# Two attentions and a mixture of experts: values placed ahead of transposes, rows split inside the head loop, scatter groups moved among products

## The reference, cut to what matters

```python
# neighbourhood attention, per head and row of the 4 x 64 grid
s = einsum(q_r, k_g) + bias
p = softmax(s)
o = einsum(p, v_g)          # 16 heads of 64; then o @ w_o
# latent attention, per head, all 256 keys
s = (q_nope . k_nope + q_rope . k_rope) * scale
o = softmax(s) @ v          # 16 heads of 64; then o @ w_o
# experts
for e in range(8):
    y = y + combine[:, e:e+1] * _swiglu(hf, w_gu[e], w_down[e])
```

## Time and profile before

| | us |
|---|---|
| median of 3 runs | 1655.73 (1654.92 to 1656.09) |
| the profiled execution, its own time | 1658.01 |
| its span, first to last instruction | 1656.2 |
| mean granted TensorE clock | 0.988 |
| PE busy | 1580.6 (95%) |
| DVE busy | 1203.5 (73%) |
| ACT busy | 866.1 (52%) |
| GpSimd busy | 116.6 (7%) |
| DMA, mean rate | 233 GB/s |

### The profile page before, as it was taken

The page is one execution under the profiler, slowest core; times in us unless marked ns, Lnnn a source line. Parts: engine busy times, 40 slices in busy tenths (PEclk is TensorE's granted clock), DMA queues, the critical chain, the costliest instruction groups (busy, mean ns, idle before and its releaser), DMA issues.

```text
span 1656.2 us, 24755 instructions
## 1 busy us (share of the span) xinstructions
PE 1580.6 (95%) x10292; PEld 1360.5 (82%) x10292; DVE 1203.5 (73%) x1428; ACT 866.1 (52%) x1009; POOL 116.6 (7%) x138
## 2 busy tenths in 40 slices
PE   7999999979999999998999999889999999999998
PEld 7999989867999989856999986578787877877876
DVE  5777769754777776455776763568888988988996
ACT  5333456443443354335434343457777677777765
POOL 0100012210000000151000002600000000000000
PEclk9999999999999999999999999999999999999999
DMA  8777634222687755404877740029998988988983
GB/s 330 276 283 263 252 105 150 71 77 76 264 324 284 297 212 177 154 1 169 304 257 279 267 178 1 1 102 351 342 344 314 375 312 317 364 323 308 365 327 134
DMA packets 51922, 386.32 MB, mean 233 GB/s; under 512 B 5888, under 2 KB 6224, under 8 KB 7904
## 3 DMA queue, kind: packets, MB, share of 16 engines
q1 hardware_dynamic: 50400, 376.16, 61.5%
q0 software_dynamic: 1408, 8.54, 1.4%
HBM read 383.63 MB, written 1.05 MB: 232 GB/s over the span
## 4 chain that ended last, share of the span: by engine, by line
PE 80%; DVE 9%; ACT 5%; issue 2%; POOL 2%; DMA 1%; DVEq 0%; ACTq 0%
PE bank L302 22%; PE bank L304 21%; PE bank L303 21%; PE bank L1286 4%; DVE sb_wlo L269 2%; PE bank L1861 1%; ACT sb_whi L265 1%; DVE sb_wlo L2288 1%; DMA sb_ada_raw<-in_ada 1%; PE bank L1820 1%; DVE sb_ada_acc L686 1%; PE bank L2016 1%; PE bank L696 1%; PE bank L540 1%; PE bank L1976 1%
## 5 line engine op out<-in xcount | busy, mean ns | idle before, releaser
L269 DVE TENSOR_TENSOR sb_wlo<-sb_raw,sb_whi 128x2048 fp32r<-128x2048 f32 x137 | 313.8, 2292 | 170.6 <-ACT sb_whi L265 170.4
L302 PE MATMUL bank<-sb_xhi,sb_whi 128*128 128x256 f32 x1344 | 382.8, 285 | 4.3 <-DVE sb_xlo L582 1.8
L303 PE MATMUL bank<-sb_xlo,sb_whi 128*128 128x256 f32 x1344 | 380.9, 283 | 0.0
L304 PE MATMUL bank<-sb_xhi,sb_wlo 128*128 128x256 f32 x1344 | 380.9, 283 | 0.0
L265 ACT ACTIVATE sb_whi<-sb_raw 128x2048 fp32r<-128x2048 f32 x137 | 261.5, 1909 | 177.1 <-PE bank L304 177.0
L302 PEld LDWEIGHTS bank<-sb_xhi,sb_whi 128*128 128x128 f32 x1344 | 258.5, 192 | 8.5 <-issue 4.0
L303 PEld LDWEIGHTS bank<-sb_xlo,sb_whi 128*128 128x128 f32 x1344 | 258.5, 192 | 1.1
L304 PEld LDWEIGHTS bank<-sb_xhi,sb_wlo 128*128 128x128 f32 x1344 | 258.5, 192 | 0.0
L2288 DVE TENSOR_TENSOR sb_wlo<-sb_raw,sb_whi 128x2048 fp32r<-128x2048 f32 x84 | 191.4, 2286 | 15.2 <-ACT sb_whi L2282 14.0
L302 PE MATMUL bank<-sb_whi,sb_slots_hi 128*128 128x512 f32 x448 | 181.5, 405 | 0.0
L304 PE MATMUL bank<-sb_whi,sb_slots_lo 128*128 128x512 f32 x448 | 176.3, 393 | 0.0
(11 more groups left out here) (462 smaller groups left out, 2492.3 us busy)
## 6 DMA issues: line engine op xcount, KB each, us to landing
sb_raw<-in_ffn SPq DMA_DIRECT2D x98, 1024.0 KB, 4.9
sb_raw<-in_moe SPq DMA_DIRECT2D x86, 1024.0 KB, 5.3
sb_ada_raw<-in_ada SPq DMA_DIRECT2D x32, 1536.0 KB, 6.3
sb_cst<-in_moe SPq DMA_DIRECT2D x28, 1024.0 KB, 5.1
sb_xn<-in_moe SPq DMA_DIRECT2D x27, 1024.0 KB, 5.2
sb_ada_raw<-in_moe SPq DMA_DIRECT2D x27, 1024.0 KB, 5.1
sb_raw<-in_w_in SPq DMA_DIRECT2D x13, 1024.0 KB, 4.8
sb_raw<-in_na_qk SPq DMA_DIRECT2D x8, 1024.0 KB, 5.3
```

Of the source, the lines that this page charges most:

```text
L269: e.tensor_tensor(wlo[s][:, :], raw[s][:, :], whi[s][:, :], ALU.subtract).then_inc(s_lo[s], 1)
L302: e.matmul(dst, wh, xh, start=first, stop=False, skip_group_check=skip)
L303: e.matmul(dst, wh, xl, start=False, stop=False, skip_group_check=skip)
L304: return e.matmul(dst, wl, xh, start=False, stop=last, skip_group_check=skip)
```

## The change

In both attentions `weigh(i - 3)` is put ahead of `transposed(i - 2)` in each iteration. The splitting of rows into high and low parts moves from behind the loop into it: k-tiles 0 to 5 in iterations 7, 11 and 15, the last two behind the loop. In the experts, piece 3 of the scatter moves behind `p_in(j + 1)` of k-steps 0 and 1 and `p_turn(j)`, and pieces 0 to 2 move behind k-steps 4 and 5. No operation is added or removed.

```diff
--- before.py
+++ after.py
@@ -324,15 +324,18 @@
             m = act.step(lambda e: e.activation(dst, src, ACT.Sqrt, bias=bias, scale=scale), *after)
             return dve.step(lambda e: e.reciprocal(dst, dst), m)
 
+        def split_pair(k, *after):
+
+            mh = act.step(lambda e: e.activation(xhi[:, k:k + 2, :], xn[:, k:k + 2, :], ACT.Copy), *after)
+            ml = dve.step(lambda e: e.tensor_tensor(xlo[:, k:k + 2, :], xn[:, k:k + 2, :], xhi[:, k:k + 2, :],
+                                                    ALU.subtract), mh)
+            return [ml, ml]
+
         def split_xn(m):
 
             parts = []
             for k in range(0, KT, 2):
-                mh = act.step(lambda e, k=k: e.activation(xhi[:, k:k + 2, :], xn[:, k:k + 2, :], ACT.Copy),
-                              *(m[k:k + 2] if isinstance(m, list) else (m,)))
-                ml = dve.step(lambda e, k=k: e.tensor_tensor(xlo[:, k:k + 2, :], xn[:, k:k + 2, :],
-                                                             xhi[:, k:k + 2, :], ALU.subtract), mh)
-                parts += [ml, ml]
+                parts += split_pair(k, *m[k:k + 2])
             return parts
 
         s_acc, s_sum, s_scaled = sem("accumulated"), sem("residual_added"), sem("gate_applied")
@@ -1867,17 +1870,23 @@
                 dst, src = order(dst), src.rearrange("p (r c) -> p r c", c=GRID)
             m_out[i // 2] = act.step(lambda e: e.activation(dst, src, ACT.Copy), m)
 
+    def split(n):
+        return env["split_pair"](2 * n, *[m_out[2 * n + z] for z in range(2)])
+
+    parts = []
     for i in range(AH + 3):
         if i < AH:
             softmax(i)
         if 0 <= i - 1 < AH:
             normalised(i - 1)
+        if 0 <= i - 3 < AH:
+            weigh(i - 3)
         if 0 <= i - 2 < AH:
             transposed(i - 2)
-        if 0 <= i - 3 < AH:
-            weigh(i - 3)
+        if i >= 7 and i % 4 == 3:
+            parts += split(i // 4 - 1)
         follow(i)
-    return [m_out[i] for i in range(AH // 2)]
+    return parts + split(AH // 4 - 1)
 
 
 def neighbourhood(env, early, m_in):
@@ -1939,7 +1948,6 @@
         m = attend(env, ctx, "na", scores, lambda i, kb: v[:, kb, i * HD:(i + 1) * HD], 1.0,
                    bias[:, :, :, :, :].rearrange("p b h r c -> p b h (r c)"), lambda i: [*m1, m_b, m_mask], follow, lambda i: (mask[i % 2 * HD:i % 2 * HD + HD, 0:P], mask[i % 2 * HD:i % 2 * HD + HD, P:P + T]),
                    lambda z: backwards(z.rearrange("p (r c) -> p r c", c=GRID)))
-        m = env["split_xn"](m)
         env["release"]()
     return env["project"](ch["na_o"], m, env["first"]["ffn3"]), kept[3]
 
@@ -2550,10 +2557,10 @@
             ex, u = j // EU, j % EU
             if gathers(j):
                 p_gather(e, *gathers(j))
+            p_in(e, j + 1, range(0, 2))
+            p_turn(e, j)
             if u == 1 and ex > 0:
                 p_scatter(e, ex - 1, (3,))
-            p_in(e, j + 1, range(0, 2))
-            p_turn(e, j)
             p_in(e, j + 1, range(2, 4))
             if u == 5:
                 p_keys(e, ex)
@@ -2564,9 +2571,10 @@
                 p_down(e, j, (1,))
                 p_down(e, j + 1)
                 break
+            p_in(e, j + 1, range(4, 6))
             if u == 0 and ex > 0:
                 p_scatter(e, ex - 1, (0, 1, 2))
-            p_in(e, j + 1, range(4, 8))
+            p_in(e, j + 1, range(6, 8))
             p_down(e, j)
         p_scatter(e, EXPERTS - 1, END)
```

## The result

The changed kernel takes 1637.07 us (median of 4 runs, 1635.96 to 1637.94); run beside it, the kernel before takes 1655.33 (1653.43 to 1656.09). The direction and most of the mechanisms came out; one mechanism, the price of the splits, did not, and the sizes were too small. One execution that fell in the chip's slower state (1740.4 at a granted clock of 0.843, of the kernel with two tensors on GpSimd) is left out of every median here.

The account below looks back on a forecast made before the run. TensorE, busy 95% of the span, was taken as the bound, so only its waits and slow stretches could be won. Attentions 6.2 plus experts 5.2 made 11.4 us, 1655.7 to 1644.3, range 1639 to 1650.

Parts of the forecast that it names:

- Values ahead, first attention: First attention: transposes no longer wait for GpSimd's normalisation in iterations 5, 7, 9, 11 and 13, 5 x 0.46 = 2.3 us.
- Values ahead, second attention: Second attention: the same waits gone, three pairs without gate rows 0.74 each, three with them 0.45 each, together 3.5 us.
- Tails: End of each attention: the projection starts 9.7 after head 15's scores instead of 10.68; 1.0 won twice, 2.0 us.
- Splits in the loop: Both attentions: inserted splits cost 1.6 us in all, DVE's low parts being held by GpSimd; bounds nothing and 9.8.
- Held until then, DVE is free at 5.06: First attention: low part held until GpSimd's normalisation ends at 4.37, DVE 0.99 late, transposes wait some 0.4 in iteration 13.
- 0.15 and 0.25: Last pair of heads in the attentions: costs counted because the reciprocal of head 15 comes late.
- Experts: Changes of expert: later scatter pieces win 1.0 in each of 4 without a gather, 0.4 in the others, 5.2 us.
- Both forecast waits: Experts: seven waits of 0.55, transposes for DVE's product, and three of about 1, gather for the addition.
- Rival (a): Experts: DVE isn't late, so 12.2 us won there and 1637.3 in all, 1641 with half the difference; chance 0.12.
- rival (d): Attention heads: changed rhythm holds PE at 1.2 GHz, so slower, 1686 us for a whole attention; chance 0.04.
- own bounds: Whole kernel: splits 0.5 to 4, pairs with gates 0 to 0.74, experts 3 to 8, giving 1640.5 to 1649 us.
- a wait behind iteration 11's split in the first attention: Transposes expected to wait 0.4 to 0.8 us two iterations behind the split of iteration 11.

Follow-up runs that it names:

- the kernel with two tensors on GpSimd: Changed kernel with GpSimd's normalisation as a product of two SBUF tensors instead of a product with a scalar per partition: 1637.06 us, ratio 0.9895.
- the run with values first only: Kernel before with only the values put ahead of the transposes, rows split behind the loop as before: 1651.23 us against 1654.19, ratio 0.9987.
- the run in which GpSimd's had that kind: Changed kernel with GpSimd's normalisation as a two-tensor multiplication, done twice for heads 6, 10 and 14: 1641.95 us, one run.
- the DVE order: Changed kernel with DVE's expert queue reordered: gate-up product ahead of piece 0's addition, piece 3's addition right behind pieces 1 and 2: 1637.49 us, ratio 0.9895.
- after again: Changed kernel run and profiled again with nothing else altered: 1637.02 us, ratio 0.9893.

## Why the prediction was wrong, step by step

It was wrong in size: 11.4 forecast, 14.6 in the traces, 18.3 between the medians. Its steps miss 3.2, the largest part being the splits; another 4 lie outside its steps, and these take the result out of the range. In the order of its steps:

- **Values ahead, first attention, 2.3.** 2.57. The three pairs without gate rows gave 0.46 each, as said; the two with them gave 0.6.
- **Values ahead, second attention, 3.5.** 4.37 (with the splits out of the way). Two terms were small: a pair without gates gave 0.89 and not 0.74, for PE's iteration turned out 2.46 and not the 2.55 counted, and pairs with gates gave 0.53 to 0.59 instead of 0.45.
- **Tails, 2.0.** 2.3. The reckoned 9.7 from the S of head 15 to the projection was 9.54 and 9.31.
- **Splits in the loop, 1.6 in all.** This is the step that failed by its mechanism. "Held until then, DVE is free at 5.06" did not happen: DVE's low part ran its 0.69 beside GpSimd's normalisation, six times of six. The low part, and the high part of ACT that it waits for, do delay what stands behind them on DVE: the reciprocal of head 11 comes 0.47 later than in the run with values first only in the first attention, where 0.60 is spare, and 0.64 later in the second. That of head 15 comes 1.06 and 0.90 later, right behind the low part, but T of head 15 stands behind a W that waits for a copy, and does not wait; 0.15 and 0.25 were counted for it. The nearest row was of another kind of GpSimd instruction (TENSOR_TENSOR in the mixer), and the run in which GpSimd's had that kind shows the hold. What was left of the cost is one wait of 0.26, with its restart 0.33, in iteration 13 of the second attention.
- **Experts, 5.2.** 5.65: 3 x 0.47 and 4 x 1.06, where 0.4 and 1.0 stood. Both forecast waits are there, in number and kind, 0.4 long and not 0.55. Rival (a) is excluded by them, and the DVE order shows what most of it would have been worth: 4.1 more.
- **The steps together** are 3.2 short: splits 1.3, second attention 0.9, tails 0.3, first attention 0.3, experts 0.4. With the traced 14.6 the forecast would have been 1641.1, inside the range.
- **The rest, 4.** The 58 runs of the kernel before beside the experiments have a median of 1654.6 and not 1655.7: 1.1. The whole change's runs had a mean clock of 0.9898 and before's 0.9879: 1.4 by the slope. Some 1.5 stay unexplained. The prediction weighed the granted clock only as a risk (rival (d), a whole attention at 1.2 GHz). It should have had a spread of 2 us to either side for it, which the "own bounds" left out. Rival (d) itself did not come: from head 5 to head 15 the granted clock is 1.00 in every profile. But the low stretch of the earlier trace rows is still there. In the window 700 to 710 the clock went from 0.66 to 0.86, only because the heads start 5.7 us earlier. Counted from the first S, the first 20 us of the heads have the same 0.83 in the first profile of the change as before, and 0.74 in the second.

Windows of 20 us from the first S: before, after, after again:

```profile
695.30:715.30 20.00, 16.25 (x66) 8.95 (x67) 8.25 (x39) 7.87 (x24) 10.39 (x11) 0.83 0.10 41
```

```profile
689.60:709.60 20.00, 16.64 (x69) 9.31 (x70) 8.58 (x39) 8.25 (x25) 10.64 (x12) 0.83 0.10 43
```

```profile
692.91:712.91 20.00, 16.64 (x63) 8.95 (x64) 7.47 (x35) 7.86 (x24) 9.48 (x11) 0.74 0.10 42
```

And the low part of iteration 15's split with the reciprocal of head 15 right behind it; after, first attention:

```profile
740.20 0.69 DVE L330 TENSOR_TENSOR sb_xlo<-sb_xn,sb_xhi 128x512 fp32r<-128x512 f32 x1 [0.37 <-ACT sb_xhi L329]
740.81 0.16 DVE L1844 RECIPROCAL sb_mx_na<-sb_mx_na 128x2 f32<-128x2 f32 x1
```

Of what the prediction wanted to see, all was seen but two things: low parts longer beside GpSimd, and a wait behind iteration 11's split in the first attention.

## What to carry to other kernels

A price for "two engines hold each other" must come from a row with the same kinds of instruction on both engines; another kind is a bound, not a price. Where differences under 5 us of 1650 are at stake, count what repeats in the trace (head to head, unit to unit) and set the granted clock of the runs beside the medians, for the medians of single parts need not add up. And when PE's order is changed, look at once at the queue of the engine that then releases it: here DVE's order in the experts held 4 us more. And set windows of two profiles at the same point of the work, not at the same microsecond: the same low clock looked higher only because it had moved.

## What the runs showed of the hardware that was not expected

- GpSimd multiplies 128x256 by a broadcast column faster as TENSOR_TENSOR (0.61) than as TENSOR_SCALAR (0.92); two in a row take 1.30 and 1.94.
- TENSOR_TENSOR on DVE and TENSOR_TENSOR on GpSimd lengthen each other by about half an instruction (0.69 to 1.08, 2.60 to 3.01); beside GpSimd's TENSOR_SCALAR DVE's TENSOR_TENSOR kept its 0.69. DVE's two-column TENSOR_SCALAR goes from 0.17 to 0.52 and 0.84 beside GpSimd's TENSOR_TENSOR, and to as much as 0.35 beside its TENSOR_SCALAR.
- Kernels with the same operations, but for GpSimd's form of one product, had mean granted clocks from 0.9858 to 0.9900 in their runs, and 0.004 goes with 3 us, as much as a part of the change. That the order of instructions causes it is not shown.
